# Adding the residual of an output projection by an accumulating transfer, issued by GpSimd, in place of a load and a VectorE add

## The chip, the cores and the metric

The kernel runs on one core of one Trainium2 chip. The metric is the device time of one execution in microseconds (us); less is better. A core has a matrix engine (TensorE, PE in the profile), a vector engine (VectorE, DVE), a scalar engine (ScalarE, ACT), a general engine (GpSimd, POOL) and a synchronising engine (SyncE, SP), which here issues all transfers. Each engine works through its own list of instructions in order, and the engines meet only through semaphores: an instruction can wait until a counter has reached a value.

## What is computed

One layer of a decoder trunk over 512 tokens of width 2048, in float32. Cut to what matters here:

```python
a = rmsnorm(x, norm_mix_w)
z = a @ w_in                                  # 33 tiles of output features
mixed = concat(ssm(z), pool(z), gla(z))       # 512 x 2048
h = x + mixed @ w_out                         # the output projection, with its residual x
f = conv_glu_ffn(rmsnorm(h, norm_ffn_w))      # up to 2 x 5632, down again
h = h + f
h = h + (p @ w_ple) * sigmoid(rmsnorm(h) @ w_pg)
out = rmsnorm(h, final_norm_w)
```

## The kernel before

Everything is held with features on the 128 partitions and the 512 tokens along them, so a 512 x 2048 activation is 16 tiles of 128 x 512. `Y` holds such an activation, `xs_hi` and `xs_lo` hold the two parts into which an activation is split so that a float32 product can be made from three matmuls (hi by hi, lo by hi, hi by lo: lines 432, 433, 434). The weights are split too: SP loads 128 x 2048 values, the weights of one output tile, into `w_raw`; ACT copies them rounded to `w_hi` (line 765); DVE subtracts and leaves the rest in `w_lo` (line 1050). There are two buffers of each, and two PSUM banks, used by turns.

A tile of the program is one output tile: 16 steps k, each of three matmuls of 128x512. The tiles are numbered through the whole kernel: 0 to 32 are the input projection, 33 (`OUT0`) to 48 are the output projection, 49 (`FFN0`) and on are the FFN. Below, residual tile j is tile 33 + j, with j from 0 to 15. The order on each engine is the order in which the code is written.

For each residual tile j, once PE has finished it (`tile_done`):

- DVE adds the PSUM bank to `x_res[:, j]` and writes `Y[:, j]` (`add_x`, line 1334; semaphore `evacuated`), splits the weights of tile j + 2 (`w_rest`), waits for ACT's square of `Y[:, j]`, and adds that square to the running sum `ss` (`add_square`, line 1079).
- ACT rounds the weights of tile j + 2 (`w_half`), then squares `Y[:, j]` (`square`, line 793).
- SP has loaded `x_res` from DRAM two tiles at a time (lines 390 and 398). `x_res` lies in memory which the mixers use before, so its first load waits for the last mixer product (`y_gla_made`).

At the end of the output projection the input of the FFN must be made from `Y`. After tile j = 15 has read the first eight parts of `xs_hi` and `xs_lo` (`front_read`), ACT makes the new `xs_hi` 0 to 7 (line 788) and DVE the new `xs_lo` 0 to 7 (line 1073), which stand in DVE's list ahead of the add for tile 15. After tile 15 is done, ACT makes `xs_hi` 8, squares `Y[:, 15]`, makes `xs_hi` 9 to 12, rounds the weights of tile 50 and makes `xs_hi` 13 to 15; DVE follows it, and adds the last square after `xs_lo` 9. In PE's list, tile 49 begins at once, and between its steps 7 and 8 stands the sum of `ss` over the partitions, for the norm of the FFN:

```python
if first and s == 0 and k == 8:
    sum_tokens(2 * KT, [ss], bank[2], sum_spread)   # line 468; waits for all 16 squares
if first and s == 1 and k == 6:
    spread(diag_made, 2, val[:], bank[2], rstd_spread)  # line 475
```

Of the kernel before, what the change touches and what calls it, by code (L numbers as in the profile page):

```python
# [21 lines left out]
P = 128  # L22
SEQ = 512
D = 2048
KT = D // P
# [13 lines left out]
HEADS = 4  # L39
# [8 lines left out]
OUT0 = IN_TILES  # L48
# [34 lines left out]
ALU = mybir.AluOpType  # L83
# [30 lines left out]
def build(nc, A):  # L114
    with ExitStack() as ctx:
        def sb(name, shape, dt=F32, where=ctx):
            return where.enter_context(nc.sbuf_tensor(name, shape, dt))

        def sem(name):
            return ctx.enter_context(nc.semaphore(name))  # L120
# [11 lines left out]
        Y = sb("Y", [P, KT, SEQ])  # L132
# [38 lines left out]
        gla.close()  # L171
        mix.close()

        outp = ExitStack()
        x_res = sb("x_res", [P, KT, SEQ], where=outp)
        outp.close()

        pg = ExitStack()
        ple = sb("ple", [P, KT, SEQ], where=pg)
        pg.close()  # L180
# [41 lines left out]
        wpool_in = sem("wpool_in")  # L222
        a2_in = sem("a2_in")
        glu_in = sem("glu_in")
        xres_in = [sem(f"xres_in{g}") for g in range(2)]
        p_in = sem("p_in")
        w_in = [sem(f"w_landed{s}") for s in range(2)]
        hi_begun = sem("hi_begun")
# [5 lines left out]
        evacuated = sem("evacuated")  # L234
# [74 lines left out]
        y_gla_made = sem("y_gla_made")  # L309
# [30 lines left out]
        def in_width(n):  # L340
            return W_G if n == N_G else W_FULL
# [12 lines left out]
        @block.sync  # L354
        def _(sp):
            def weights(c, e, src, width, free=True):
                if free:
                    sp.wait_ge(lo_made, 2 * e + c - 1)
                sp.dma_start(w_raw[c % 2][:, 0:width], src).then_inc(w_in[c % 2], 16)

            for n in range(IN_TILES):
                src = A["w_in_g"] if n == N_G else A["w_in"][n - (n > N_G)]
                if n == 0:
                    sp.dma_start(params[:], A["params"]).then_inc(params_in, 16)
                    for g in range(4):
                        gs = slice(X_GROUPS[g], X_GROUPS[g + 1])
                        sp.dma_start(Y[:, gs, :], A["x"][:, gs, :]).then_inc(x_in[g], 16)
                        if g == 0:
                            weights(n, 0, src, D, free=False)
                else:  # L370
                    weights(n, 0, src, in_width(n), free=n >= 2)
                if n == 1:
                    sp.dma_start(ident[:], A["ident"]).then_inc(s5_in, 16)
                    sp.dma_start(iota_t, A["iota"]).then_inc(s5_in, 16)
                    for c in range(2):
                        sp.dma_start(B_in[c], A["s5_b"][:, c, :]).then_inc(s5_in, 16)
                    sp.dma_start(CM[:], A["s5_c"]).then_inc(s5_in, 16)
                    sp.dma_start(causal[:], A["causal"]).then_inc(a2_in, 16)
                    sp.dma_start(w_a2[:], A["w_a2"]).then_inc(a2_in, 16)
                    sp.dma_start(corr[:], A["corr"]).then_inc(a2_in, 16)  # L380
                if n == HEAD_SLOT + 2:
                    sp.wait_ge(states_made, PAIRS)
                    sp.dma_start(Y[:, 12:16, :], A["w_glu"]).then_inc(glu_in, 16)
                if n == HEAD_SLOT + 5:
                    sp.wait_ge(glu_done, 4)
                    sp.dma_start(w_pool, A["w_pool"]).then_inc(wpool_in, 16)
            for s in range(2):
                weights(OUT0 + s, 0, A["w_out"][s], W_FULL)
            sp.wait_ge(y_gla_made, 2 * HEADS)
            sp.dma_start(x_res[:, 0:2, :], A["x"][:, 0:2, :]).then_inc(xres_in[0], 16)  # L390

            def out_pair(j, r):

                i = 2 * j + r
                for s in range(2):
                    weights(OUT0 + s, i, A["w_out"][2 * i + s], W_FULL)
                two = slice(2 * i, 2 * i + 2) if isinstance(i, int) else bass.ds(2 * i, 2)
                sp.dma_start(x_res[:, two, :], A["x"][:, two, :]).then_inc(xres_in[r % 2], 16)

            with sp.Fori(0, KT // 4 - 1) as j:  # L400
                out_pair(j, 1)
                out_pair(j, 2)
            out_pair(KT // 4 - 1, 1)
            with sp.Fori(0, QUARTERS) as q:
                with sp.Fori(0, QT) as i:
                    for s in range(2):
                        weights(FFN0 + s, q * HALF_Q + i, A["w_up"][q * UP + 2 * i + s], W_FULL)
                with sp.Fori(0, KT // 2) as i:
                    for s in range(2):
                        weights(FFN0 + UP + s, q * HALF_Q + i, A["w_down"][q * KT + 2 * i + s], W_DOWN)  # L410
            sp.wait_ge(mid_lo_made, FT)
            for k in range(PLE_KT):
                sp.dma_start(p_raw[k], A["p"][:, k, :]).then_inc(p_in, 16)
            for s in range(2):
                weights(PLE0 + s, 0, A["w_ple"][s], W_FULL)
            with sp.Fori(0, KT // 2) as i:
                for s in range(2):
                    weights(PG0 + s, i, A["w_pg"][2 * i + s], W_FULL)
            for t in range(KT):

                from_pool = t % 3 == 2 and t // 3 < POOL_OUT
                j = t // 3 if from_pool else POOL_OUT + t - min((t + 1) // 3, POOL_OUT)
                sp.wait_ge(*((out_pool_made, j + 1) if from_pool else (out_made, j + 1 - POOL_OUT)))
                sp.dma_start(A["out"][:, j, :], Y[:, j, :]).then_inc(written, 16)
            sp.wait_ge(written, 16 * KT)
# [328 lines left out]
        def _(act):  # L754
# [6 lines left out]
            def w_half(c, e=0, width=W_FULL, used=0):  # L761

                landed(act, c, e)
                act.wait_ge(tile_done, 2 * e + (c - 1 - used))
                nc.scalar.activation(w_hi[c % 2][:, 0:width], w_raw[c % 2][:, 0:width], ACT.Copy).then_inc(hi_made, 1)  # L765
# [16 lines left out]
            def w_first(c):  # L782
                landed(act, c)
                nc.scalar.activation(w_hi[c % 2][:], w_raw[c % 2][:], ACT.Copy).then_inc(hi_made, 1)

            def x_half(k, gain=None):
                scale = 1.0 if gain is None else par(gain, k)
                nc.scalar.activation(xs_hi[:, k, :], Y[:, k, :], ACT.Identity, scale=scale).then_inc(xs_hi_made, 1)

            def square(src, used, made):  # L790
                act.wait_ge(evacuated, made)
                act.wait_ge(sq_used, used)
                nc.scalar.activation(sq[:], src, ACT.Square).then_inc(squared, 1)
# [102 lines left out]
            for n in range(2, IN_TILES):  # L896
                s = n - HEAD_SLOT
# [54 lines left out]
            with act.Fori(0, KT // 2 - 1) as i:  # L952
                for s in range(2):
                    w_half(OUT0 + 2 + s, i)
                    square(Y[:, bass.ds(2 * i + s, 1), :], 2 * i + (KT + s), 2 * i + (OUT0 + s + 1))
            w_half(FFN0)
            square(Y[:, KT - 2, :], 2 * KT - 2, FFN0 - 1)
            act.wait_ge(front_read, KT // 2)
            for k in range(KT):
                if k == KT // 2:  # L960
                    act.wait_ge(tile_done, FFN0)
                x_half(k, "ffn")
                if k == KT // 2:
                    square(Y[:, KT - 1, :], 2 * KT - 1, FFN0)
                if k == KT - 4:
                    w_half(FFN0 + 1)
# [72 lines left out]
        def _(dve):  # L1039
            tt, ts, stt = nc.vector.tensor_tensor, nc.vector.tensor_scalar, nc.vector.scalar_tensor_tensor  # L1040
# [228 lines left out]
            for n in range(2, IN_TILES):  # L1269
                s = n - HEAD_SLOT  # L1270
# [54 lines left out]
            def add_x(j_pair, r, s, follow, square=True):  # L1325

                i = 2 * j_pair + r
                j = 2 * i + s
                if s == 0:
                    dve.wait_ge(xres_in[r], 16 * j_pair + 16)  # L1330
                dve.wait_ge(tile_done, j + (OUT0 + 1))
                row = (lambda a: a[:, j, :]) if isinstance(i, int) else (lambda a: a[:, bass.ds(j, 1), :])
                out = bank[(OUT0 + s) % 2][:] if isinstance(i, int) else bank[(OUT0 + s) % 2][:].unsqueeze(1)
                tt(row(Y), row(x_res), out, ALU.add).then_inc(evacuated, 1)
                if follow is not None:
                    w_rest(*follow)
                if square:
                    add_square(j + KT)
# [124 lines left out]
        def _(pool):  # L1463
            tt, ts = nc.gpsimd.tensor_tensor, nc.gpsimd.tensor_scalar
# [94 lines left out]
                tt(Y[:, 8 + k, :], Y[:, 8 + k, :], QKV[:, 8 + k, :], ALU.mult).then_inc(y_gla_made, 1)  # L1559


            pool.wait_ge(scaled, POOL_OUT)
            pool.wait_ge(rstd_made, 4)
            for j in range(POOL_OUT):
# [88 lines left out]
```

## Time and profile before

| | us |
|---|---|
| time, median of 3 runs | 2410.23 |
| lowest and highest of them | 2408.67 and 2410.54 |
| span of the profiled execution | 2409.5 |
| PE busy in it | 2333.4 (97%) |
| DVE busy in it | 1213.0 (50%) |
| ACT busy in it | 766.0 (32%) |
| POOL busy in it | 226.4 (9%) |

For the profiled execution the span from its first to its last instruction is given, and no time of its own beside it; the median of the runs is 0.7 us above that span. PE is busy nearly all the time, and the other engines have idle time in every tile. A matmul of 128x512 is shown with some 390 ns, but they overlap: the next one starts 0.227 us after the one before.

### The profile page before, as it was taken

The numbers are of one execution on the slowest core, as the hardware profiler recorded it, in microseconds if no ns is written. First come the engines' busy times: TensorE is split into PE (matmuls) and PEld (weight loads), VectorE is DVE, ScalarE is ACT, GpSimd is POOL, SyncE is SP. The second block draws the span as 40 slices with busy tenths as digits, with TensorE's granted clock in tenths as the row PEclk, the third lists the DMA queues.
The fourth block names the chain that finished last, engine by engine and source line by source line (L and its number), as shares of the span: only waits on it lengthen the run. The fifth ranks groups of instructions, "written<-read, shape, count | busy, mean of one in ns | idle before, by whom it ended". The sixth has DMA issues, their size and how long they took to land.

```text
span 2409.5 us, 26555 instructions
## 1 busy us (share of the span) xinstructions
PE 2333.4 (97%) x10176; PEld 1873.3 (78%) x10176; DVE 1213.0 (50%) x1287; ACT 766.0 (32%) x774; POOL 226.4 (9%) x174
## 2 busy tenths in 40 slices
PE   8987989999999999999999999999999999999996
PEld 6754667887888888888888888888888888888884
DVE  6899984455336444334444434444434444436444
ACT  5311215444225333223333223333222222226432
POOL 3366560400000000000000000000000000000001
PEclk9998999999999999999999999999999999999997
DMA  5111111213322222222222223222222222232221
GB/s 220 70 48 60 53 70 71 75 53 114 127 108 87 104 98 82 91 95 104 104 90 91 85 100 104 104 87 94 84 101 104 104 87 94 84 110 105 91 101 70
DMA packets 37383, 224.39 MB, mean 93 GB/s; under 512 B 4289, under 2 KB 4801, under 8 KB 17121
## 3 DMA queue, kind: packets, MB, share of 16 engines
q1 hardware_dynamic: 37344, 223.88, 26.2%
q8 instruction: 24, 0.39, 0.1%
q14 instruction: 15, 0.11, 0.0%
HBM read 219.67 MB, written 4.19 MB: 93 GB/s over the span
## 4 chain that ended last, share of the span: by engine, by line
PE 91%; DVE 6%; issue 1%; POOL 0%; ACT 0%; DMA 0%; DVEq 0%; SPq 0%; POOLq 0%; ACTq 0%
PE bank L432 29%; PE bank L433 29%; PE bank L434 29%; DVE w_lo L1050 1%; PE bank L523 1%; PE bank L468 0%; PE bank L508 0%; DVE xs_lo L1071 0%; DVE QKV L1143 0%; DVE QKV L1144 0%; PE bank L603 0%; DVE Y L1459 0%; PE bank L509 0%; DVE QKV L1141 0%; DVE QKV L1142 0%
## 5 line engine op out<-in xcount | busy, mean ns | idle before, releaser
L432 PE MATMUL bank<-xs_hi,w_hi 128*128 128x512 f32 x2432 | 957.7, 394 | 11.8 <-DVE w_lo L1057 10.4
L433 PE MATMUL bank<-xs_lo,w_hi 128*128 128x512 f32 x2432 | 949.2, 390 | 0.0
L434 PE MATMUL bank<-xs_hi,w_lo 128*128 128x512 f32 x2432 | 949.2, 390 | 0.0
L765 ACT ACTIVATE w_hi<-w_raw 128x2048 fp32r<-128x2048 f32 (+1 forms) x214 | 375.1, 1753 | 867.4 <-PE bank L434 859.6
L1050 DVE TENSOR_TENSOR w_lo<-w_raw,w_hi 128x2048 fp32r<-128x2048 f32 (+1 forms) x216 | 461.9, 2139 | 185.2 <-ACT w_hi L765 182.2
L432 PEld LDWEIGHTS bank<-xs_hi,w_hi 128*128 128x128 f32 x2432 | 457.9, 188 | 118.5 <-issue 11.9
L433 PEld LDWEIGHTS bank<-xs_lo,w_hi 128*128 128x128 f32 x2432 | 457.9, 188 | 96.0 <-issue 2.6
L434 PEld LDWEIGHTS bank<-xs_hi,w_lo 128*128 128x128 f32 x2432 | 457.7, 188 | 95.6
L432 PE MATMUL bank<-mid_hi,w_hi 128*128 128x512 f32 x704 | 278.4, 395 | 0.0
L434 PE MATMUL bank<-mid_hi,w_lo 128*128 128x512 f32 x704 | 278.4, 395 | 0.0
L433 PE MATMUL bank<-mid_lo,w_hi 128*128 128x512 f32 x704 | 278.4, 395 | 0.0
L1565 POOL TENSOR_TENSOR Y<-Y,rstd 128x512 f32<-128x512 f32 x5 | 8.4, 1716 | 1832.3 <-ACT rstd L1035 1832.3
L1398 DVE TENSOR_TENSOR Y<-Y,bank 128x512 f32 (+1 forms) x64 | 44.0, 688 | 254.2 <-PE bank L434 254.2
L434 PEld LDWEIGHTS bank<-mid_hi,w_lo 128*128 128x128 f32 x704 | 132.2, 188 | 32.1
L433 PEld LDWEIGHTS bank<-mid_lo,w_hi 128*128 128x128 f32 x704 | 132.2, 188 | 32.1
L432 PEld LDWEIGHTS bank<-mid_hi,w_hi 128*128 128x128 f32 x704 | 132.2, 188 | 32.0
L1365 DVE TENSOR_TENSOR conv_in<-bank,rstd 128x512 f32<-128x512 f32 x44 | 30.5, 693 | 201.0 <-PE bank L434 197.2
L1374 DVE TENSOR_TENSOR val<-bank,rstd 128x512 f32<-128x512 f32 x44 | 30.4, 692 | 193.3 <-PE bank L434 193.2
L980 ACT ACTIVATE mid_hi<-val 128x512 f32 (+1 forms) x44 | 27.8, 632 | 231.7 <-DVE val L1377 231.7
L977 ACT ACTIVATE silu_g<-conv_acc 128x512 f32<-128x512 f32 x44 | 27.9, 633 | 161.4 <-DVE conv_acc L1370 161.4
L812 ACT ACTIVATE Y<-QKV 128x512 f32<-128x512 f32 x16 | 10.1, 631 | 207.9 <-DVE QKV L1145 193.1
L1079 DVE TENSOR_TENSOR ss<-ss,sq 128x512 f32<-128x512 f32 x95 | 65.2, 686 | 13.2 <-ACT sq L1024 13.2
(235 smaller groups left out, 1519.7 us busy)
## 6 DMA issues: line engine op xcount, KB each, us to landing
w_raw<-in_w_up SPq DMA_DIRECT2D x88, 1024.0 KB, 4.8
w_raw<-in_w_down SPq DMA_DIRECT2D x64, 704.0 KB, 4.0
w_raw<-in_w_in SPq DMA_DIRECT2D x32, 1024.0 KB, 4.8
w_raw<-in_w_out SPq DMA_DIRECT2D x16, 1024.0 KB, 4.8
w_raw<-in_w_pg SPq DMA_DIRECT2D x16, 1024.0 KB, 4.8
x_res<-in_x SPq DMA_DIRECT2D x8, 512.0 KB, 5.6
out_h<-Y SPq DMA_DIRECT2D x16, 256.0 KB, 2.3
Y<-in_x SPq DMA_DIRECT2D x2, 1280.0 KB, 12.3
```

Source lines behind the costliest of these rows:

```text
L432: nc.tensor.matmul(out, w_h, x_h, start=first, stop=False)
L433: nc.tensor.matmul(out, w_h, x_l, start=False, stop=False)
L434: return nc.tensor.matmul(out, w_l, x_h, start=False, stop=last)
L523: m = nc.tensor.matmul(bank[(6, 7, 5, 5)[j]][:], Y[:, 12 + k, j * P:(j + 1) * P], Y[:, k, :], start=k == 0, stop=k == S5_TILES - 1)
L765: nc.scalar.activation(w_hi[c % 2][:, 0:width], w_raw[c % 2][:, 0:width], ACT.Copy).then_inc(hi_made, 1)
L977: nc.scalar.activation(silu_g[:], conv_acc[:], ACT.Silu).then_inc(silu_made, 1)
L980: nc.scalar.activation(dst, val[:], ACT.Copy).then_inc(mid_hi_made, 1)
L1050: tt(w_lo[c % 2][:, 0:width], w_raw[c % 2][:, 0:width], w_hi[c % 2][:, 0:width].bitcast(F32), ALU.subtract).then_inc(lo_made, 1)
L1079: tt(ss[:], ss[:], sq[:], ALU.add).then_inc(sq_used, 1)
L1365: tt(conv_in[:, 2:], bank[FFN0 % 2][:], rstd[:], ALU.mult).then_inc(evacuated, 1)
L1374: tt(val[:], bank[(FFN0 + 1) % 2][:], rstd[:], ALU.mult).then_inc(evacuated, 1)
L1398: tt(y, y, out, ALU.add).then_inc(evacuated, 1)
```

## The change

The tile buffer `x_res` and its eight loads on SP go. DVE only copies the PSUM bank to `Y[:, j]`. Then GpSimd, which waits for that copy (`evacuated`), issues a transfer for each tile that adds `x[:, j]` from DRAM onto `Y[:, j]` (256 KB each, 16 of them). Two semaphores `x_added` tell that it has landed, and ACT waits for them before it reads `Y[:, j]`. The diff:

```diff
-        outp = ExitStack()
-        x_res = sb("x_res", [P, KT, SEQ], where=outp)
-        outp.close()
...
-            sp.wait_ge(y_gla_made, 2 * HEADS)
-            sp.dma_start(x_res[:, 0:2, :], A["x"][:, 0:2, :]).then_inc(xres_in[0], 16)
-            def out_pair(j, r):
-                i = 2 * j + r
+            with sp.Fori(1, KT // 2) as i:
                 for s in range(2):
                     weights(OUT0 + s, i, A["w_out"][2 * i + s], W_FULL)
-                two = slice(2 * i, 2 * i + 2) if isinstance(i, int) else bass.ds(2 * i, 2)
-                sp.dma_start(x_res[:, two, :], A["x"][:, two, :]).then_inc(xres_in[r % 2], 16)
...
+            def residual_in(i, s):
+                act.wait_ge(x_added[s], 16 * i + 16)
...
             with act.Fori(0, KT // 2 - 1) as i:
                 for s in range(2):
                     w_half(OUT0 + 2 + s, i)
+                    residual_in(i, s)
                     square(Y[:, bass.ds(2 * i + s, 1), :], 2 * i + (KT + s), 2 * i + (OUT0 + s + 1))
             w_half(FFN0)
+            residual_in(KT // 2 - 1, 0)
             square(Y[:, KT - 2, :], 2 * KT - 2, FFN0 - 1)
...
                 x_half(k, "ffn")
                 if k == KT // 2:
+                    residual_in(KT // 2 - 1, 1)
                     square(Y[:, KT - 1, :], 2 * KT - 1, FFN0)
...
-                if s == 0:
-                    dve.wait_ge(xres_in[r], 16 * j_pair + 16)
                 dve.wait_ge(tile_done, j + (OUT0 + 1))
...
-                tt(row(Y), row(x_res), out, ALU.add).then_inc(evacuated, 1)
+                nc.vector.tensor_copy(row(Y), out).then_inc(evacuated, 1)
...
+            def add_residual(i, s):
+                j = 2 * i + s
+                pool.wait_ge(evacuated, j + (OUT0 + 1))
+                row = (lambda a: a[:, j, :]) if isinstance(i, int) else (lambda a: a[:, bass.ds(j, 1), :])
+                pool.dma_start(row(Y), row(A["x"]), accum_op=ALU.add).then_inc(x_added[s], 16)
+            for s in range(2):
+                add_residual(0, s)
+            with pool.Fori(1, KT // 2) as i:
+                for s in range(2):
+                    pool.wait_ge(x_added[s], 16 * i)
+                    add_residual(i, s)
```

The order of ACT's instructions at the end of the output projection, where it turns to the input of the FFN. Before, from the weights of tile 49 on (line 793 is the square of a tile of `Y`, line 788 makes a part of `xs_hi`):

```order
L765 ACTIVATE w_hi<-w_raw 128x2048 [waits tile_done,w_landed1]
L793 ACTIVATE sq<-Y 128x512 [waits sq_used,evacuated]
L788 ACTIVATE xs_hi<-Y,params_sb 128x512 [waits front_read]
L788 ACTIVATE xs_hi<-Y,params_sb 128x512 x7
L788 ACTIVATE xs_hi<-Y,params_sb 128x512 [waits tile_done]
L793 ACTIVATE sq<-Y 128x512 [waits sq_used,evacuated]
L788 ACTIVATE xs_hi<-Y,params_sb 128x512 x4
L765 ACTIVATE w_hi<-w_raw 128x2048 [waits tile_done,w_landed0]
L788 ACTIVATE xs_hi<-Y,params_sb 128x512 x3
```

The same place in the changed kernel:

```order
L749 ACTIVATE w_hi<-w_raw 128x2048 [waits tile_done,w_landed1]
L781 ACTIVATE sq<-Y 128x512 [waits sq_used,evacuated,x_added0]
L776 ACTIVATE xs_hi<-Y,params_sb 128x512 [waits front_read]
L776 ACTIVATE xs_hi<-Y,params_sb 128x512 x7
L776 ACTIVATE xs_hi<-Y,params_sb 128x512 [waits tile_done]
L781 ACTIVATE sq<-Y 128x512 [waits sq_used,evacuated,x_added1]
L776 ACTIVATE xs_hi<-Y,params_sb 128x512 x4
L749 ACTIVATE w_hi<-w_raw 128x2048 [waits tile_done,w_landed0]
L776 ACTIVATE xs_hi<-Y,params_sb 128x512 x3
```

Nothing moves on ACT, but the squares of tiles 14 and 15, with all that stands behind them, now wait for `x_added` too.

POOL's list had nothing between its last product for the mixers and its share of the output (lines 1548 and 1569 of the changed kernel). Now sixteen transfers stand there, two and then seven times two in a loop:

```order
L1548 TENSOR_TENSOR Y<-Y,QKV 128x512 [waits r_silu]
L1556 DMA Y<-in_x 128x512 [waits evacuated] x2
L1560 UNCONDITIONAL_BRANCH
L1560 ISA
L1554 ISA [waits x_added0]
L1556 ISA [waits evacuated]
L1556 DMA Y<-in_x 128x512
L1554 REGISTER_ALU [waits x_added1]
L1556 ISA [waits evacuated]
L1556 DMA Y<-in_x 128x512
L1560 REGISTER_ALU
L1560 COMPARE_AND_BRANCH
```

Each of them waits for DVE's copy of its tile, and from the third on for the transfer of two tiles before.

## Rows read from the trace of the kernel before

**Rows 1.** The page: busy time by engine, and the chain that ended last.

```profile
PE 2333.4 (97%) x10176; PEld 1873.3 (78%) x10176; DVE 1213.0 (50%) x1287; ACT 766.0 (32%) x774; POOL 226.4 (9%) x174
...
PE 91%; DVE 6%; issue 1%; POOL 0%; ACT 0%; DMA 0%; DVEq 0%; SPq 0%; POOLq 0%; ACTq 0%
```

**Rows 2.** Groups by line and shape, output projection (560 to 731 us): busy, mean ns | idle before.

```profile
L432 PE MATMUL bank<-xs_hi,w_hi 128*128 128x512 f32 x249 | 97.2, 391 | 1.3 <-DVE w_lo L1050 0.7 <-DVE xs_lo L1071 0.6
...
L1334 DVE TENSOR_TENSOR Y<-x_res,bank 128x512 f32 x12 | 8.3, 688 | 66.7 <-PE bank L434 66.3 <-DVE ss L1322 0.5
```

**Rows 3.** Timeline of DVE, tiles 14 and 15: start, duration, idle time before.

```profile
720.06 0.69 DVE L1334 TENSOR_TENSOR Y<-x_res,bank 128x512 f32<-128x512 f32 x1 [6.14 <-PE bank L434]
721.97 2.29 DVE L1050 TENSOR_TENSOR w_lo<-w_raw,w_hi 128x2048 fp32r<-128x2048 f32 x1 [1.22 <-ACT w_hi L765]
...
726.23 5.39 DVE L1073 SCALAR_TENSOR_TENSOR xs_lo<-Y,params_sb,xs_hi 128x512 fp32r<-128x512 f32 x8 [1.37 <-ACT xs_hi L788]
731.53 0.68 DVE L1334 TENSOR_TENSOR Y<-x_res,bank 128x512 f32<-128x512 f32 x1
...
734.19 0.68 DVE L1079 TENSOR_TENSOR ss<-ss,sq 128x512 f32<-128x512 f32 x1
...
739.78 2.29 DVE L1050 TENSOR_TENSOR w_lo<-w_raw,w_hi 128x2048 fp32r<-128x2048 f32 x1
```

**Rows 4.** Timeline of ACT, same stretch.

```profile
721.84 0.61 ACT L793 ACTIVATE sq<-Y 128x512 f32<-128x512 f32 x1
725.40 5.02 ACT L788 ACTIVATE xs_hi<-Y,params_sb 128x512 fp32r<-128x512 f32 x8 [2.95 <-PE bank L434]
730.84 0.73 ACT L788 ACTIVATE xs_hi<-Y,params_sb 128x512 fp32r<-128x512 f32 x1 [0.42 <-PE bank L434]
732.25 0.63 ACT L793 ACTIVATE sq<-Y 128x512 f32<-128x512 f32 x1 [0.68 <-DVE Y L1334]
```

**Rows 5.** Timeline of PE: tile 49's start, the sum, tile 50's start, the spread.

```profile
730.64 0.39 PE L432 MATMUL bank<-xs_hi,w_hi 128*128 128x512 f32 x1
...
736.08 0.95 PE L468 MATMUL bank<-ones,ss 128*128 128x1 f32 x8
...
742.42 0.39 PE L432 MATMUL bank<-xs_hi,w_hi 128*128 128x512 f32 x1
...
746.50 1.02 PE L475 MATMUL bank<-val,ones 128*128 128x512 f32 x2
```

**Rows 6.** Issues of transfers: count, KB each, median us to landing.

```profile
x_res<-in_x SPq DMA_DIRECT2D x8, 512.0 KB, 5.6
out_h<-Y SPq DMA_DIRECT2D x16, 256.0 KB, 2.3
...
Y<-in_w_pool SPq DMA_DIRECT2D x1, 256.0 KB, 2.6
```

**Rows 7.** The tile `x_res`: landing of its eight loads, and their issue.

```profile
L398 SPq DMA_DIRECT2D x_res<-in_x x7: 347/348/432, 568.0 to 692.0; - x7
...
DMA to landing us min/median/max: 3.5/5.6/6.2
```

**Rows 8.** POOL's last work for the mixers: min/median/max ns.

```profile
L1559 POOL TENSOR_TENSOR Y<-Y,QKV x2: 1615/1684/1754, 555.0 to 558.7; 128x512 f32<-128x512 f32 x2
```

**Rows 9.** The tile `S`: DVE copies out of PSUM, min/median/max ns.

```profile
L1212 DVE COPY S<-bank x4: 424/424/425, 411.4 to 522.2; 128x256 f32<-128x256 f32 x4
```

**Rows 10.** PE in the state-space stretch, after waits, and its granted clock (last but two).

```profile
114.19 1.02 PE L508 MATMUL bank<-st_re,CM 128*32 128x512 f32 x2 [3.16 <-POOL st_im L1535]
132.91 1.62 PE L508 MATMUL bank<-st_re,CM 128*32 128x512 f32 x2 [4.15 <-POOL st_im L1535]
...
114.00:118.00 4.00, 3.81 (x12) 1.00 0.00 0
...
133.00:137.00 4.00, 4.00 (x7) 0.57 0.00 0
137.00:141.00 4.00, 4.00 (x18) 1.00 0.00 0
```

More of the change, by code:

```diff
@@ L224, in build @@
         glu_in = sem("glu_in")
-        xres_in = [sem(f"xres_in{g}") for g in range(2)]
+        x_added = [sem(f"x_added{g}") for g in range(2)]
         p_in = sem("p_in")
@@ L388, in _ @@
                 weights(OUT0 + s, 0, A["w_out"][s], W_FULL)
-            sp.wait_ge(y_gla_made, 2 * HEADS)
-            sp.dma_start(x_res[:, 0:2, :], A["x"][:, 0:2, :]).then_inc(xres_in[0], 16)
-            def out_pair(j, r):
-                i = 2 * j + r
+            with sp.Fori(1, KT // 2) as i:
                 for s in range(2):
                     weights(OUT0 + s, i, A["w_out"][2 * i + s], W_FULL)
-                two = slice(2 * i, 2 * i + 2) if isinstance(i, int) else bass.ds(2 * i, 2)
-                sp.dma_start(x_res[:, two, :], A["x"][:, two, :]).then_inc(xres_in[r % 2], 16)
[L400 to L403, printed above, removed]
             with sp.Fori(0, QUARTERS) as q:
```

## The prediction

> **What bounds the kernel now.** I read the page first: PE is busy for 97% of the span and makes 91% of the chain that ended last [rows 1]. So DVE and ACT work costs nothing as long as PE does not wait for it, and each microsecond for which PE newly waits is a microsecond of the result. Next I read the groups inside the output projection. In 171 us PE idles 1.3 us, both times at its start, for `xs_lo` and `w_lo`, neither of which the change touches; DVE idles 66.7 us before twelve of its adds, each time until PE has finished a tile [rows 2]. Inside the stage there is nothing to win, and much room. The seam between the output projection and the FFN is different. There PE starts tile 49 at 730.64 and after eight steps, at 736.08, takes the sum of `ss` [rows 5], and that sum needs the square of tile 15, which needs the add of tile 15, begun only at 731.53 [rows 3]. So I read the seam on three engines.
>
> **The seam before.** DVE's add of tile 15 ends at 731.53 + 0.69 = 732.22. ACT begins the square at 732.25 [rows 4]. DVE adds it to `ss` from 734.19 to 734.87 [rows 3]. PE takes the sum at 736.08 without having waited: room 1.2 us. The weights of tile 50 come out of the same chain: ACT makes `xs_hi` 9 to 12, then rounds these weights, DVE's `w_lo` follows and ends at 739.78 + 2.29 = 742.07 [rows 3], and tile 50 starts at 742.42 [rows 5]: room 0.35 us, 0.3 us after a hand-over of 0.05. ACT works without a gap from the square to that point, so all of this moves with the square.
>
> **The change, part by part.** Removed: eight issues on SP, 0.35 us each [rows 7], on a queue for which PE never waits in this stage [rows 2]: 0. The first of them stood behind the wait for the last mixer product, and the weights of tile 35 behind it; since PE does not wait for `w_lo` of tile 35, that is 0 too. The DVE add becomes a copy: 0.69 us before [rows 2]; the nearest row is a copy of half the length, 0.42 us [rows 9], so 0.42 to 0.69 and, as twice the elements add, near 0.65. In tiles 0 to 14 this lies in DVE's idle time, and at tile 15 it gives 0.04 us, which I leave out.
>
> Added: call L the time from the end of DVE's copy until the landed transfer lets ACT go. It holds the hand-over to POOL, POOL's issue, 256 KB of `x` added onto 256 KB of `Y`, and the semaphore. POOL issues no transfer in the trace of before and none there adds, so L is bounded by neighbours. From below, nothing can be had for less than a plain 256 KB transfer from SP: 2.3 us for stores, 2.6 us for a load [rows 6]. From above, the slowest neighbours together: the median load of 512 KB beside a load of weights, 5.6 us [rows 6], and a whole product on POOL for the issue, 1.7 us [rows 8]: 7.3 us. For the value I take, the transfer must read as many bytes as a 512 KB load, and at the seam no load of weights runs beside it, which is the least of the eight loads, 3.5 us [rows 7]; POOL's issue is between SP's 0.35 us and 1.7 us, so 1.0. That gives L = 4.5 us.
>
> The Trainium skill (DMA: Bandwidth & Descriptors, section on the anatomy of one DMA on the GpSimd path) fits such a transfer with 2.0 us plus its bytes at 436 GB/s, an estimate of 2.6 us here, and by the formula below 2.3 us of loss. No run so far shows it for an adding transfer. The Trainium skill (Collectives: The Full Stack, the bandwidth ceiling in Part 3) says that in the collectives an adding transfer reads two sources and ran at half the rate of a copy, which speaks for the dearer side.
>
> In tiles 0 to 13, L is hidden. After a copy that ends at E, the `w_lo` that DVE makes next ends at 724.26 - 720.75 = 3.5 us, as before, because it stands ahead of the square in DVE's list. The square ends at E + L + 0.61, its addition 0.68 later. DVE's next add begins at E + 3.5 + 0.68 + 6.14 = E + 10.3 [rows 3], so L may be up to 10.3 - 1.3 = 9.0 us before a tile is late. POOL has nothing else there, and only the next transfer stands behind its wait.
>
> At tile 14, ACT's square waits until 720.75 + L and ends 0.61 later. Behind it stand `xs_hi` 0 to 7, which now begin at 725.40 because they wait for PE [rows 4]. They begin later only if 721.36 + L is over 725.40, that is L over 4.0. Then DVE's `xs_lo` 0 to 7 and the copy of tile 15 behind them are later by m = L - 4.0; DVE goes from these straight into tile 15's add, with no idle time noted [rows 3]. For L = 4.5, m = 0.5 us.
>
> At tile 15, nothing hides L. The square begins at 732.25 + m + L. `ss` is ready at 734.87 + 0.05 + m + L, so PE waits at the sum for L + m - 1.15 = 3.85 us. `w_lo` of tile 50 is ready at 742.07 + m + L, and PE would get there at 742.42 + 3.85; it waits again until the whole shift is L + m - 0.3 = 4.7 us. That is the loss, and nothing gives it back: the norm's later steps (root, spread at 746.50 [rows 5]) hang on the same instructions and move with them, and PE has no idle time after the seam to take them into.
>
> The granted clock comes on top. Rows of the state-space stretch show PE after waits of similar length. After 3.16 us the clock stayed at 1.00, that is 2.4 GHz. After 4.15 us the four microseconds from 133 show a mean of 0.57, that is nearly all at 1.2 GHz, and then 1.00 again [rows 10]. At half speed for 0.43 x 4 / 0.5 = 3.4 us PE loses 1.7 us. The wait of 3.85 us here is nearer to the second, so I count it. It falls into tile 49, where PE would wait for `w_lo` anyway, so the two do not add: the shift is the larger of 4.7 and 3.85 + 1.7 = 5.55 us. The sum is against the profiled span, 2409.5 + 5.5 = 2415.0, and the median lies 0.7 above that span, so 2415.7 us. A measurement of this kernel tells about 0.2% from no change, here 4.8 us; my forecast lies just beyond it.
>
> **The rivals.**
>
> A, the transfer is quick, L from 2.3 to 3.5 us. This ends on the other side, as no measurable change. Then m = 0, the wait at the sum is 1.15 to 2.35 us, shorter than the 3.16 us after which the clock held, and the loss is 2.0 to 3.2 us: 2412.2 to 2413.4. Plain transfers of this size speak for it [rows 6]; against it, they do not read their target and are not issued by POOL. Together with the clock it decides at L of about 4.1, where 4.8 us is reached with a clock fall, or 4.55 without one. Chance 0.32.
>
> B, the forecast, L from 3.5 to 5.0: without a fall of the clock 3.2 to 5.7 us, with one up to 6.55. So 2413.4 to 2416.8. Chance 0.42, of which I put 0.15 on less than 4.8 us.
>
> C, the transfer is slow, L from 5.0 to 9.0: both ends of the seam count, L twice. At 5.6 us the loss is 2 x 5.6 - 4.3 = 6.9 us and with the clock 7.75; at 7.3 us it is 10.3, with the clock 11.15, so up to 2421.4. For it: an adding transfer is unlike any row. Against: POOL's list and all 16 DMA engines are free there. Chance 0.20.
>
> D, L over 9.0: every tile is late. At 10 us, DVE slips by 1.0 us at each of 15 tiles, PE has 730.64 - 724.26 = 6.4 us of room before it waits for `w_lo`, so 8.6 us, and the seam's 2 x 10 - 4.3 = 15.7 on top: some 2434. Nothing in the profile speaks for it. Chance 0.03.
>
> E, faster: with fewer loads on SP the stage's first weights come sooner. PE's 0.7 us wait for `w_lo` [rows 2] would have to come from that, but those weights were loaded long before, and DVE was still at `xs_lo`. At most -0.7 us even so; only a gain that I don't see would be over 0.2%. Chance 0.03, of which 0.02 faster.
>
> **How the numbers follow.** No measurable change: 0.32 (A) + 0.15 (B) + 0.01 (E) = 0.48. Slower: 0.27 (B) + 0.20 (C) + 0.03 (D) = 0.50. Faster: 0.02. The time is that of B. The range goes down to the lowest bound of A, 2412.2, and up to the upper bound of L in C with the clock, 2421.4; outside lie D, E and the ends of A and C beyond their bounds, below 0.2 together.
>
> **What the profile of the changed kernel would show.** PE waits before line 468's counterpart in tile 49 for 3.85 us, and for `w_lo` before tile 50 for about 0.8 us if the clock holds (none if it falls). The wait between the copy of tile 15 and ACT's square is L, 4.5 us, and the landing of the sixteen transfers from their issue about 3.5 us. DVE's idle time before the copies in tiles 0 to 14 stays near 6 us, the copy takes about 0.65 us, and the granted clock shows 0.5 for some 3 us right after 736. I am wrong if L is under 3.5 us, if it is over 5 us, or if PE waits for a transfer inside the stage.

## The result, and the profile after

The changed kernel takes 2417.01 us (median of 6 runs), the kernel before 2410.92 us in the same comparison. The ratio is 1.0025, with a 95% interval from 1.0014 to 1.0036: slower by 6.1 us. The interval lies above 1, but 0.25% is little more than the 0.2% that the prediction took for the least that can be told.

The page of the changed kernel, its busy times, its queues (packets, MB, and the time of the packets as a share of the span of the 16 engines) and its chain (to be read beside [rows 1]):

```profile
PE 2345.2 (97%) x10176; PEld 1880.0 (78%) x10176; DVE 1214.5 (50%) x1287; ACT 767.7 (32%) x774; POOL 241.7 (10%) x190
...
q1 hardware_dynamic: 36192, 219.69, 25.4%
q0 software_dynamic: 2304, 4.20, 1.1%
...
PE 91%; DVE 6%; issue 1%; DMA 1%; POOL 0%; ACT 0%; DVEq 0%; SPq 0%; POOLq 0%; ACTq 0%
```

The page of before has one queue:

```profile
q1 hardware_dynamic: 37344, 223.88, 26.2%
```

The 4.20 MB of the residual moved from this queue to GpSimd's. POOL is busier by 15 us, mostly the sixteen issues; DVE is not less busy, although it only copies now. "DMA 1%" is new in the chain: a transfer stands on the path that sets the end.

Where, the waits of PE between 731 and 750 us tell (engine, line, what it waited for: us in total, times, longest). From the second tile of the output projection up to 2300 us PE has no other wait:

```profile
PE bank L452 <- DVE ss L1070: 3.8, 1, 3.8
```

PE waits at the sum of `ss` (line 452 now). The timeline of DVE, of POOL and of ACT over the same place, to be read beside [rows 3] and [rows 4]:

```profile
718.77 0.69 DVE L1323 COPY Y<-bank 128x512 f32<-128x512 f32 x1 [4.05 <-PE bank L418]
...
724.77 0.69 DVE L1070 TENSOR_TENSOR ss<-ss,sq 128x512 f32<-128x512 f32 x1 [1.77 <-ACT sq L781]
725.50 5.39 DVE L1064 SCALAR_TENSOR_TENSOR xs_lo<-Y,params_sb,xs_hi 128x512 fp32r<-128x512 f32 x8
730.81 0.68 DVE L1323 COPY Y<-bank 128x512 f32<-128x512 f32 x1
...
737.30 0.75 DVE L1064 SCALAR_TENSOR_TENSOR xs_lo<-Y,params_sb,xs_hi 128x512 fp32r<-128x512 f32 x1 [5.15 <-ACT xs_hi L776]
737.97 0.68 DVE L1070 TENSOR_TENSOR ss<-ss,sq 128x512 f32<-128x512 f32 x1
```

```profile
732.16 0.86 POOL L1556 DMA_DIRECT2D Y<-in_x  x1 [11.17 <-DVE Y L1323]
```

```profile
724.11 0.63 ACT L781 ACTIVATE sq<-Y 128x512 f32<-128x512 f32 x1 [3.43 <-DMA Y<-in_x]
724.64 5.66 ACT L776 ACTIVATE xs_hi<-Y,params_sb 128x512 fp32r<-128x512 f32 x9
736.03 0.63 ACT L781 ACTIVATE sq<-Y 128x512 f32<-128x512 f32 x1 [5.72 <-DMA Y<-in_x]
```

The copy of tile 15 ends at 730.81 + 0.68 = 731.49, POOL begins to issue 0.67 us later, and ACT's square begins at 736.03. So L is 4.54 us at tile 15 and, by the same reading, 724.11 - 719.46 = 4.65 us at tile 14. The sixteen issues, by the tile `in_x` (min/median/max ns), and the median of their landing, 3.9 us after the issue began, by the page's issues:

```profile
L1556 POOL DMA_DIRECT2D Y<-in_x x16: 853/862/1057, 567.9 to 732.2; - x16
```

```profile
Y<-in_x POOLq DMA_DIRECT2D x16, 256.0 KB, 3.9
```

The copy takes 0.69 us, as the add did.

Behind the wait the clock falls. Stretches of 2 us: PE's busy time and instructions, granted clock, share and rate of the DMA engines:

```profile
736.00:738.00 2.00, 0.00 (x0) 1.00 0.00 0
738.00:740.00 2.00, 1.20 (x6) 0.55 0.00 0
740.00:742.00 2.00, 2.00 (x7) 0.50 0.00 0
742.00:744.00 2.00, 2.00 (x6) 0.50 0.00 0
744.00:746.00 2.00, 2.00 (x8) 0.75 0.00 0
746.00:748.00 2.00, 2.00 (x11) 1.00 0.39 94
```

From 738.8, when PE goes on, until 745 it runs at 0.50, that is 1.2 GHz: 6.2 us at half speed, 3.1 us lost. The mean of 0.55 from 738 to 740 puts the fall itself at 738.2, when PE still waited.

To weigh whole seams against each other I measure from the start of tile 14's copy (or add) to the start of the spread of the norm (line 459 now), which is one fixed piece of work. Before it is 746.50 - 720.06 = 26.44 us [rows 3, 5]; here the spread starts at

```profile
752.27 1.02 PE L459 MATMUL bank<-val,ones 128*128 128x512 f32 x2
```

and 752.27 - 718.77 = 33.50 us. The seam costs 7.06 us in this execution. Its span is only 5.4 us longer, 2414.9 against 2409.5. It reached tile 14's copy 1.29 us earlier, and it was already 1.4 us ahead at the first tile of the output projection, where the change begins; the remaining 0.4 us it gained behind the seam.

### The profile page after: what moved, and what is told of

It reads as the page before. It is cut to its first block, busy times and chain, and to the rows that moved or that the text cites. A ratio compares the mean times of both kernels' runs of the same rounds, so it can differ in the third digit from the quotient of the medians.

```text
span 2414.9 us, 26645 instructions
## 1 busy us (share of the span) xinstructions
PE 2345.2 (97%) x10176; PEld 1880.0 (78%) x10176; DVE 1214.5 (50%) x1287; ACT 767.7 (32%) x774; POOL 241.7 (10%) x190
## 3 DMA queue, kind: packets, MB, share of 16 engines
q0 software_dynamic: 2304, 4.20, 1.1%
## 4 chain that ended last, share of the span: by engine, by line
PE 91%; DVE 6%; issue 1%; DMA 1%; POOL 0%; ACT 0%; DVEq 0%; SPq 0%; POOLq 0%; ACTq 0%
PE bank L416 29%; PE bank L417 29%; PE bank L418 29%; DVE w_lo L1041 1%; PE bank L507 1%; PE bank L492 1%; PE bank L452 1%; DVE xs_lo L1062 0%; PE bank L493 0%; PE bank L587 0%; DVE Y L1448 0%; DVE QKV L1134 0%; DVE QKV L1135 0%; DVE QKV L1132 0%; PE bank L582 0%
```

## The experiments

The four kernels of the second to the fifth line ran on one chip (before: 2411.96 us there), the last four on another (before: 2411.82 us there). L, the time from the end of DVE's copy to ACT's square, and the seam are read as above; m is what the time from DVE's write of tile 14 to its write of tile 15 has over the 731.53 - 720.06 = 11.47 us of before. L, the wait and the seam come from one trace of each kernel.

| kernel | median us | ratio, 95% interval | L at tile 15 | PE's wait at the sum | seam longer by |
|---|---|---|---|---|---|
| changed | 2417.01 | 1.0025 [1.0014, 1.0036] | 4.54 | 3.8 | 7.06 |
| tile 15 loaded | 2413.58 | 1.0006 [0.9997, 1.0015] | none | 0 | 0.54 |
| only tile 15 adds | 2417.13 | 1.0023 [1.0014, 1.0032] | 4.75 | 3.5 | 5.40 |
| reordered | 2412.30 | 1.0000 [0.9991, 1.0009] | 4.69, hidden | 0 | 0.03 |
| 17 matmuls more | 2416.03 | 1.0018 [1.0009, 1.0027] | 4.68 | 0.4 | 5.50 |
| changed, again | 2418.73 | 1.0029 [1.0017, 1.0041] | 4.78 | 4.3 | 7.79 |
| later transfers | 2421.92 | 1.0044 [1.0030, 1.0057] | 6.83 | 7.6 | 10.77 |
| 8 matmuls more | 2418.22 | 1.0028 [1.0017, 1.0040] | 4.85 | 2.3 | 6.04 |
| plain transfers | 2416.68 (one run) | | 3.53 | 2.3 | 3.37 |

### Tile 15 loaded and added by DVE

```diff
+            sp.dma_start(x_last[:], A["x"][:, KT - 1, :]).then_inc(xlast_in, 16)
...
-                    residual_in(KT // 2 - 1, 1)
...
+                if square:
                     nc.vector.tensor_copy(row(Y), out).then_inc(evacuated, 1)
+                else:
+                    dve.wait_ge(xlast_in, 16)
+                    tt(row(Y), x_last[:], out, ALU.add).then_inc(evacuated, 1)
```

> The changed kernel, but the residual of tile 15 alone is loaded ahead and added by DVE as before; tiles 0 to 14 keep their adding transfers. Theory 1 (the whole loss is the unhidden latency behind the last tile, with the clock fall that it brings): PE no longer waits at the sum of ss, the granted clock stays at 1.00 after it, and the time is that of before, plus up to 0.3 us because tile 14's transfer still makes the xs_hi behind it 0.5 us late: 2411 us. Theory 2 (the sixteen transfers cost something each, in POOL's list, on the DMA engines or in PE's clock, wherever they are): 15 of 16 parts of the loss stay, 2416 to 2417 us.

With fifteen of the sixteen adding transfers left, the time is not to be told from before. Its interval is 2411.2 to 2415.6 us in this set: it holds Theory 1's 0.3 us above before (2412.3) and leaves out Theory 2's 2416. In the seam PE waits 0.2 us, for `w_lo` of tile 50, and not at the sum, and the clock stays at 1.00. It is the leftover of tile 14's transfer: m is 0.67 us, so by m - 0.3 the shift is 0.4 us, and the seam is longer by 0.54. From the waits of PE:

```profile
PE bank L423 <- DVE w_lo L1047: 0.2, 1, 0.2
```

### Only tile 15 adds by transfer

```diff
-                tt(row(Y), row(x_res), out, ALU.add).then_inc(evacuated, 1)
+                if square:
+                    tt(row(Y), row(x_res), out, ALU.add).then_inc(evacuated, 1)
+                else:
+                    nc.vector.tensor_copy(row(Y), out).then_inc(evacuated, 1)
...
+                    act.wait_ge(x_added, 16)
                     square(Y[:, KT - 1, :], 2 * KT - 1, FFN0)
...
+            pool.wait_ge(evacuated, FFN0)
+            pool.dma_start(Y[:, KT - 1, :], A["x"][:, KT - 1, :], accum_op=ALU.add).then_inc(x_added, 16)
```

> The kernel before, but tile 15 alone gets its residual by an adding transfer issued by GpSimd (its load of x_res stays and isn't used). Theory 1: the wait at the sum is 4.5 - 1.15 = 3.4 us (tile 14 is on time, so no 0.5 us from it), the clock falls for 4 to 7 us after it, and the time is 5 to 6 us above before: 2415.5 to 2417 us. Theory 2: one of sixteen transfers, 0.4 us: 2411.3 us.

One adding transfer in the kernel before brings back 5.2 us of loss (2417.13 us, as many above before as Theory 1 said). PE's timeline shows the wait at the place and of the size expected:

```profile
740.90 1.02 PE L469 MATMUL bank<-ones,ss 128*128 128x1 f32 x8 [3.50 <-DVE ss L1081]
```

The clock fell behind it:

```profile
742.00:744.00 2.00, 2.00 (x7) 0.68 0.00 0
744.00:746.00 2.00, 2.00 (x6) 0.50 0.00 0
746.00:748.00 2.00, 2.00 (x10) 0.97 0.00 0
```

That is some 3.4 us at half speed, less than the 4 to 7 us expected, and half of what the changed kernel shows. Together with the run before, the loss sits behind the last tile, and nowhere else.

### The changed kernel, with the last residual needed later

```diff
-                x_half(k, "ffn")
-                if k == KT // 2:
+                if k == KT - 1:
                     residual_in(KT // 2 - 1, 1)
                     square(Y[:, KT - 1, :], 2 * KT - 1, FFN0)
+                x_half(k, "ffn")
...
-                if k == KT // 2 + 1:
+                if k == KT - 2:
                     add_square(2 * KT - 1)
...
-                        if first and s == 0 and k == 8:
+                        if first and s == 0 and k == 14:
                             sum_tokens(2 * KT, [ss], bank[2], sum_spread)
```

> The changed kernel with all sixteen adding transfers, but with nothing behind the last one that PE needs soon: ACT squares tile 15 just ahead of xs_hi 15, not ahead of xs_hi 9, DVE adds that square after xs_lo 14, and PE takes the sum of ss ahead of step 14 of tile 49, not of step 8. Theory 1: the latency stays 4.5 us, but PE doesn't wait; time of before within 1 us, 2410 to 2412. Theory 2: as the changed kernel, 2417 us. Theory 3 (the transfers cost nothing, the clock fall comes from another cause at this place): the clock falls again somewhere behind 730 us, 2413 to 2415 us.

All sixteen transfers are there, L is 4.69 us as ever, and the time is that of before. ACT's timeline at the seam shows how. It makes `xs_hi` up to 14 and rounds the weights of tile 50 while the transfer runs, and then waits 0.44 us for it, for which PE does not wait:

```profile
727.85 8.07 ACT L776 ACTIVATE xs_hi<-Y,params_sb 128x512 fp32r<-128x512 f32 x13
735.82 1.90 ACT L749 ACTIVATE w_hi<-w_raw 128x2048 fp32r<-128x2048 f32 x1
737.63 1.32 ACT L776 ACTIVATE xs_hi<-Y,params_sb 128x512 fp32r<-128x512 f32 x2
739.38 0.63 ACT L781 ACTIVATE sq<-Y 128x512 f32<-128x512 f32 x1 [0.44 <-DMA Y<-in_x]
```

PE has no wait from 720 to 765 us, and in that stretch the clock never leaves 1.00. This is the version to keep if `x_res` has to go. It does not beat the kernel before, in whose trace PE has no wait here that could be taken away. Theory 3 falls too.

### PE filled while it would wait

```diff
+                            for _ in range(17):
+                                nc.tensor.matmul(bank[3][:], w_hi[FFN0 % 2][:, 0:P], xs_hi[:, 0, :], start=True,
+                                                 stop=True)
                             sum_tokens(2 * KT, [ss], bank[2], sum_spread)
```

> The changed kernel with 17 more matmuls of 128x512 on PE ahead of the sum of ss (their result goes to an unused bank and is read by nobody); 17 x 0.227 = 3.85 us, as long as PE's wait. If the clock fall is caused by PE's idle time and costs time beside the wait: no wait at the sum, the clock stays at 1.00, PE then waits for w_lo of tile 50 for some 0.8 us, and the seam costs 4.7 us instead of 7.0: 2 us less than the changed kernel, 2414.5 to 2415.5. If the clock fall costs nothing (the rival, since w_lo of tile 50 would have been late anyway): the time is that of the changed kernel, 2417 us.

The wait at the sum shrinks to 0.4 us and the clock stays. PE's waits, and then two stretches of 2 us:

```profile
PE bank L416 <- DVE w_lo L1044: 0.6, 1, 0.6
PE bank L452 <- DVE ss L1073: 0.4, 1, 0.4
```

```profile
740.00:742.00 2.00, 1.69 (x11) 1.00 0.00 0
742.00:744.00 2.00, 2.00 (x10) 1.00 0.00 0
```

The seam costs 5.50 us, against 7.06 and 7.79 in the two profiles of the changed kernel. The second wait, for `w_lo` of tile 50, is the one that the prediction named for the case that the clock holds. L + m - 0.3, the shift without a fall of the clock, is 4.68 + 0.97 - 0.3 = 5.35 us here, and the seam is 0.15 above it; for the two profiles of the changed kernel it is 4.81 and 5.30, and their seams are 2.2 and 2.5 us above it. So the fall of the clock adds more than 2 us to the shift. The median of 2416.03 us is above the 2414.5 to 2415.5 expected, which was reckoned from a before 1 us quicker than the one on this chip. The medians, 4.1 us above before here and 6.1 and 6.9 there, point the same way, but their intervals overlap, so it is the traces that show the clock's share.

### The changed kernel again

> The changed kernel as it is, so that the others of this set are compared with it on the same chip. All theories: 5 to 7 us above before; a wait of 3.8 us at the sum of ss and a fall of the clock behind it.

PE waits 4.3 us and not 3.8, since L was 4.78 and m 0.82 us here (L + m - 1.15 = 4.45); the clock is at 0.50 from 742.0 to 748.8 us. The loss is 6.9 us.

### Every transfer 1.7 us later

The operands of the product are set once ahead of the sixteen issues, which is left out here, and so is the loop, which was written in another form with the same sense.

```diff
+                link(tt(conv_acc[:], conv_acc[:], silu_g[:], ALU.mult))
                 pool.dma_start(row(Y), row(A["x"]), accum_op=ALU.add).then_inc(x_added[s], 16)
```

> The changed kernel with a product of 128x512 on GpSimd ahead of each of the sixteen issues (its operands are used by nobody), which makes every transfer about 1.7 us later. Theory 1 in its full form (from 4.0 us on the latency counts twice, once behind tile 14 by way of the xs_hi and xs_lo ahead of tile 15's copy, once behind tile 15): L about 6.2 us, the copy of tile 15 2.2 us late, the wait at the sum 7.3 us, the seam 8.2 us without the clock and 9 to 11 us with it, so 2420 to 2422 us. Rival (it counts once, behind tile 15 only): 1.7 us above the changed kernel, 2418.7 us. Tiles 0 to 13 make PE wait in neither, since 6.2 us is below 9.0.

The median is 2421.92 us, inside the 2420 to 2422 of the full form. The rival's 1.7 us above the changed kernel is 2420.4 in this set, and that is inside the interval as well (2419.1 to 2425.6), so the time alone does not decide. The trace does. DVE's copies of tiles 14 and 15, and PE at the sum:

```profile
719.47 0.69 DVE L1323 COPY Y<-bank 128x512 f32<-128x512 f32 x1 [2.47 <-PE bank L418]
...
732.97 0.68 DVE L1323 COPY Y<-bank 128x512 f32<-128x512 f32 x1
```

```profile
743.25 1.84 PE L452 MATMUL bank<-ones,ss 128*128 128x1 f32 x8 [7.57 <-DVE ss L1070]
```

From copy to copy it is 13.50 us, against 11.47 before: m = 2.03 us. L was 6.11 us at tile 14, where POOL's product took 1.29 us, and 6.11 - 4.0 = 2.1; at tile 15 the product took 1.71 us, and L was 6.83. The wait at the sum should be L + m - 1.15 = 6.83 + 2.03 - 1.15 = 7.7, and is 7.6. So what L has over 4.0 us counts twice, once behind tile 14 and once behind tile 15. The clock was low from 739.2 to 749.4 us, 6.2 us of it after PE had gone on, as in the changed kernel. As forecast, PE has no wait in tiles 1 to 14, although every transfer is late.

### 8 matmuls in place of 17

> As the run with 17 more matmuls on PE ahead of the sum, but 8 of them: 1.8 us of work, so that PE still waits for some 2 to 2.5 us. If only a longer idle time makes the clock fall (it held at a wait of 3.16 us in the trace of before, and fell in the changed kernel at 3.8 us), it holds at 1.00 and the time is that with 17 matmuls, 2 us under the changed kernel. If any wait at this place does it, the clock falls and the time is that of the changed kernel.

This went against the expectation. PE waited only 2.3 us, shorter than the 3.16 us after which the clock had held in the trace of before [rows 10], and the clock fell all the same, for 3.4 us in place of 6.8. PE's timeline at the sum, and the stretches of 2 us around it:

```profile
741.59 1.05 PE L452 MATMUL bank<-ones,ss 128*128 128x1 f32 x8 [2.32 <-DVE ss L1073]
```

```profile
740.00:742.00 2.00, 0.41 (x4) 1.00 0.00 0
742.00:744.00 2.00, 2.00 (x11) 0.73 0.00 0
744.00:746.00 2.00, 2.00 (x6) 0.50 0.00 0
746.00:748.00 2.00, 2.00 (x9) 0.91 0.00 0
```

In time it cannot be told from the changed kernel of the same set (2418.22 and 2418.73), nor from one 2 us under it, since its interval is 2415.9 to 2421.5 us. What went against the expectation is the clock in the trace.

The traces show why the length of one wait in one trace does not settle this. The wait of 3.16 us after which the clock held [rows 10] stands in code that no kernel here changes, and it is there in all ten traces, 3.16 to 3.19 us long. The clock held behind it in two of them and fell in eight. In the first profile of the changed kernel:

```profile
114.11 1.89 PE L492 MATMUL bank<-st_re,CM 128*32 128x512 f32 x2 [3.18 <-POOL st_im L1524]
```

```profile
114.00:118.00 4.00, 3.89 (x7) 0.63 0.00 0
```

In that stretch of the kernels no wait of PE between 1.5 and 2.0 us was followed by a fall, each one over 3.7 us was, and those between went either way. So the fall behind 2.32 us here, and its absence behind 2.29 us in the next run, may be differences between two executions and not between two kernels.

### Transfers that do not add

```diff
-                pool.dma_start(row(Y), row(A["x"]), accum_op=ALU.add).then_inc(x_added[s], 16)
+                pool.dma_start(row(Y), row(A["x"])).then_inc(x_added[s], 16)
```

> The changed kernel with transfers that overwrite Y with x and do not add, 256 KB each, still issued by GpSimd; this leaves the output projection out of the result. It prices the adding. If reading the target is what costs, landing is 2.6 to 2.9 us from the issue and not 3.8, L is 3.3 to 3.6 us, and the wait at the sum 2.2 to 2.5 us. If GpSimd's way of issuing is the whole price, landing stays at 3.8 us and L at 4.5 us.

The issue is shorter, as the tile `in_x` shows (min/median/max ns, below), and the transfers land 2.8 (least) or 3.0 us (median) after it began. They carry the same 4.20 MB in 1280 packets and not 2304, and the packets' time is half as long (0.6% against 1.1%). After these two come PE's timeline at the sum and the clock:

```profile
L1556 POOL DMA_DIRECT2D Y<-in_x x16: 536/536/772, 571.3 to 735.0; - x16
```

```profile
q0 software_dynamic: 1280, 4.20, 0.6%
```

```profile
740.67 1.02 PE L452 MATMUL bank<-ones,ss 128*128 128x1 f32 x8 [2.29 <-DVE ss L1070]
```

```profile
742.00:744.00 2.00, 2.00 (x11) 1.00 0.00 0
```

So adding costs 1.0 us of L against the first profile of the changed kernel, and 1.25 us against the one of this set (4.78), of which 0.33 us is POOL's longer issue (0.86 against 0.54). Whether the rest is the reading of the target or the addition, no run separates. The clock stayed at 1.00 behind this wait of 2.29 us in this trace, and the seam is longer by 3.37 us, where L + m - 0.3 gives 3.53 + 0.04 - 0.3 = 3.27. The one time, 2416.68 us, is 4.9 us above before and more than that: this execution reached tile 14's copy at 722.17, 2.1 us later than the profiled one of before. One run cannot price 3.4 us.

## Why the prediction was right

**The place.** It said that nothing is won or lost in tiles 0 to 14 and that the whole loss sits at the seam. Shown from both sides by the kernel that loads tile 15 and the kernel that only there uses a transfer, and by the reordered one.

**L.** Taken as 4.5 us, measured 4.54 (4.78 in the second profile). That the sum came out is in part luck: I had 1.0 us for the issue and 3.5 us behind it, and it is 0.67 us of hand-over from DVE to POOL and 3.9 us from the start of the issue to the landing, of which 0.86 us is the issue. One term was too large by about what the other was too small.

**The double count and the sum.** m was taken as 0.5 and measured as 12.04 - 11.47 = 0.57 us. L + m - 1.15 gives 3.96 us for the wait at the sum, and it was 3.8 (4.45 and 4.3 in the second profile). L + m - 0.3, the seam while the clock holds, gives 5.35 for the kernel with 17 matmuls (m 0.97), where 5.50 was measured, and 3.27 for plain transfers, where 3.37 was.

**The clock.** The fall was called because 3.85 us is nearer to a wait of 4.15 us than to one of 3.16 us [rows 10]. It came, and no wait over 3.7 us in the seam or in the state-space stretch of these traces was without one, but two waits were thin ground for it: the clock fell after 2.32 us behind 8 matmuls more, and in eight of ten traces after the very wait that held it in the rows. For the same reason A's sum, which has no fall of the clock because its waits are under 3.16 us, was not safe. The term was also mis-sized: 3.4 us at half speed, 1.7 us lost, where the profile shows 6.2 us and 3.1 us lost (the second profile 6.8 us, 3.4 lost); the 3.4 us came only where a single tile adds and with 8 matmuls more. In its other half the step held: the clock's loss and the wait for `w_lo` of tile 50 do not add, and in the changed kernel that wait is gone. So the seam was 7.06 us and not 5.55. The median moved by only 6.1 us, and 6.9 us in the second comparison. The forecast of 5.5 us above before (2415.7) was low by the clock's term, within the range; that the median came as near to it as 0.6 us, when the seam is 1.5 us longer than the forecast has it, is luck too. With 0.48 on no measurable change and 0.50 on slower, the prediction did not lean far to either side.

**What was off.** I said that DVE's idle time before the copies would stay near 6 us. It is 4.05 us before tile 14's copy, and 1.77 us more stand before the addition of the square: DVE now waits in two places. The sum, 5.8 us, nearly stays, which is why nothing came of it. The copy was to take 0.65 us and takes 0.69; I had left that gain out.

**The rivals.** A quick transfer (A) is what plain ones would have been: at 3.53 us they are at its upper end, and a seam longer by 3.4 us is below the 4.8 us that the prediction took for measurable, though its one run cannot show that. The 2.6 us that the prediction gives as an estimate for such a transfer is near the plain one's 2.8 to 3.0 us and 1.3 us short of the adding one's 3.9. C's arithmetic, L counted twice, is what the later transfers followed. D and E were not seen.

## What to carry to other kernels

A transfer that takes the place of an add on an idle engine is free wherever the result is not needed for the next few microseconds (here an L of 6.1 us was still hidden inside the stage), and costs nearly its whole latency at the last tile of a stage, where the next stage waits for it. So look at the last tile first, find every instruction that stands in program order behind the new wait, and move those that do not need the result ahead of it; here three moved lines gave back the whole loss. Where the matrix engine is the bound, count a possible fall of its clock behind each new wait as a cost of its own: here it was nothing behind a wait of 2.3 us in one trace and 1.7 us behind one of 2.3 us in another, and 3.1 to 3.4 us behind waits of 3.8 to 7.6 us.

## What the runs showed of the hardware

- An adding transfer of 256 KB issued by GpSimd landed 3.9 to 4.2 us after its issue began (the medians of the traces; the one of the kernel where only tile 15 adds took 4.4), a plain one 2.8 to 3.0 us; the issue took 0.86 us and 0.54 us, the first of a kernel 1.06 and 0.77. Sixteen adding ones took 2304 packets, sixteen plain ones 1280. POOL began the issue 0.67 us after DVE's copy had ended where the wait stood in a loop, and 0.32 us after where it stood in straight code.
- DVE takes 0.69 us to copy 128x512 float32 out of PSUM, no less than for adding a second operand from SBUF.
- The length of PE's wait does not tell by itself whether the clock falls. It held at 1.00 after a wait of 2.29 us (plain transfers) and 3.16 us [rows 10], and fell after 2.32 us (8 matmuls more). The same wait of 3.16 to 3.19 us in unchanged code was followed by a fall in eight traces of ten. What tells these apart stays open.
- Nor does the fall come at a fixed place. Read from the mean clock of the stretches in the seam, it fell 0.6 us before PE went on in the changed kernel and 4.0 us before with later transfers, but 1.8 us after where only tile 15 adds and 1.3 us after with 8 matmuls more. Once down it stayed down for 3.4 us in these last two, for 6.8 us in both profiles of the changed kernel, and for 10.2 us with later transfers.
